# Sliding-window attention: transposes of the probabilities issued singly between the dense chunk's last matmuls, and VectorE's normalising moved ahead of the next maxima

## The reference, cut to what matters

```python
def sink_softmax(s, sink):
    m = jnp.maximum(jnp.max(s, axis=-1, keepdims=True), sink)
    e = jnp.exp(s - m)
    return e / (jnp.sum(e, axis=-1, keepdims=True) + jnp.exp(sink - m))

def swa_prompt(q, k, v, rel_bias, sinks):
    ...
    sc = jnp.einsum('bcqkgd,bcjkd->bckgqj', qc, k_band, preferred_element_type=jnp.float32) * SCALE
    sc = sc + rel_bias_heads(rel, rel_bias)
    ...
    p = sink_softmax(sc, sinks.astype(jnp.float32).reshape(SWA_KV_HEADS, SWA_GROUP, 1, 1))
    o = jnp.einsum('bckgqj,bcjkd->bcqkgd', p.astype(v.dtype), v_band)
```

## Time before, and the profile before

| what | value |
|---|---|
| median of 3 runs | 1555.41 us (1554.9 to 1557.6) |
| the profiled execution, first to last instruction | 1553.1 us |
| TensorE busy | 1495.8 us (96%) |
| VectorE busy | 1020.4 us (66%) |
| ScalarE busy | 607.5 us (39%) |
| GpSimd busy | 611.0 us (39%) |
| share of the chain that ended last | TensorE 80%, VectorE 9%, DMA 3%, GpSimd 3%, ScalarE 2% |

### The profile page before, as it was taken

The page is one execution under the profiler, slowest core; times in us unless marked ns, Lnnn a source line. Parts: engine busy times, 40 slices in busy tenths (PEclk is TensorE's granted clock), DMA queues, the critical chain, the costliest instruction groups (busy, mean ns, idle before and its releaser), DMA issues.

```text
span 1553.1 us, 25753 instructions
## 1 busy us (share of the span) xinstructions
PE 1495.8 (96%) x9803; PEld 1397.5 (90%) x9803; DVE 1020.4 (66%) x2016; ACT 607.5 (39%) x1256; POOL 611.0 (39%) x407
## 2 busy tenths in 40 slices
PE   6999999999999999999999999999999999999997
PEld 5889999999997998899788999999999999778885
DVE  6866667767674357867445896555555555578986
ACT  5143534435342235666223333333333332444463
POOL 6522232222222322225231568888888781000104
PEclk9999999999999999999999999999999999999999
DMA  6232222222132721129431122222222228723568
GB/s 199 63 94 74 74 87 65 73 70 70 30 97 75 233 95 38 56 82 291 156 108 58 45 67 86 83 83 83 70 83 68 71 83 278 240 97 116 170 195 156
DMA packets 156475, 165.41 MB, mean 107 GB/s; under 512 B 14005, under 2 KB 121913, under 8 KB 156353
## 3 DMA queue, kind: packets, MB, share of 16 engines
q1 hardware_dynamic: 119689, 109.34, 22.6%
q10 hardware_dynamic: 34840, 51.14, 10.0%
q0 software_dynamic: 1824, 3.28, 1.5%
HBM read 125.56 MB, written 39.85 MB: 107 GB/s over the span
## 4 chain that ended last, share of the span: by engine, by line
PE 80%; DVE 9%; DMA 3%; POOL 3%; ACT 2%; issue 2%; ACTq 1%; SPq 0%; DVEq 0%; POOLq 0%
PE bank L1138 16%; PE bank L1140 16%; PE bank L1139 16%; PE bank L1144 6%; PE bank L1146 6%; PE bank L1145 6%; PE bank L1170 4%; PE bank L1279 2%; PE bank L1250 1%; PE bank L1249 1%; DVE p L2649 1%; DVE rowsn L2408 1%; DVE p L2625 1%; POOL ring_l L1080 1%; PE bank L1629 1%
## 5 line engine op out<-in xcount | busy, mean ns | idle before, releaser
L1138 PE MATMUL bank<-ht_h,ring_h 128*128 128x352 f32 x816 | 268.9, 330 | 1.8 <-POOL ring_l L961 1.1
L1140 PE MATMUL bank<-ht_h,ring_l 128*128 128x352 f32 x816 | 263.2, 323 | 0.0
L1139 PE MATMUL bank<-ht_l,ring_h 128*128 128x352 f32 x816 | 262.6, 322 | 0.0
L960 POOL TENSOR_TENSOR ring_h<-raw,att 128x1024 fp32r<-128x1024 f32 x42 | 86.5, 2059 | 405.6 <-PE bank L1140 396.8
L1138 PE MATMUL bank<-m_h,ring_h 128*128 128x264 f32 x648 | 184.2, 284 | 1.2 <-DVE m_l L2895 1.2
L1139 PE MATMUL bank<-m_l,ring_h 128*128 128x264 f32 x648 | 184.2, 284 | 0.0
L1140 PE MATMUL bank<-m_h,ring_l 128*128 128x264 f32 x648 | 183.9, 284 | 0.0
L1138 PEld LDWEIGHTS bank<-ht_h,ring_h 128*128 128x128 f32 x816 | 153.8, 189 | 5.3 <-issue 2.0
L1139 PEld LDWEIGHTS bank<-ht_l,ring_h 128*128 128x128 f32 x816 | 154.6, 189 | 0.7
L1140 PEld LDWEIGHTS bank<-ht_h,ring_l 128*128 128x128 f32 x816 | 153.9, 189 | 0.0
L1138 PE MATMUL bank<-tb_h,ring_h 128*128 128x264 f32 x456 | 129.9, 285 | 0.2 <-DVE u2s L2909 0.2
(11 more groups left out here) (383 smaller groups left out, 3844.9 us busy)
## 6 DMA issues: line engine op xcount, KB each, us to landing
raw<-in_w_up SPq DMA_DIRECT2D x44, 512.0 KB, 3.9
raw<-in_w_in SPq DMA_DIRECT2D x34, 512.0 KB, 3.9
rb<-in_w_down SPq DMA_DIRECT2D x66, 256.0 KB, 2.9
d_y<-conv SPq DMA_DIRECT2D x22, 529.0 KB, 3.3
d_gate<-gst ACTq DMA_DIRECT2D x48, 176.0 KB, 1.9
a<-d_y SPq DMA_DIRECT2D x33, 256.0 KB, 6.1
ra<-d_y SPq DMA_DIRECT2D x33, 256.0 KB, 3.1
gm<-d_gate ACTq DMA_DIRECT2D x8, 528.0 KB, 4.4
```

Source lines behind the costliest of these rows:

```text
L960: order.link(nc.gpsimd.tensor_tensor(high, src, zero.to_broadcast(list(src.shape)), ALU.add))
L1138: nc.tensor.matmul(out, wh, xh, start=start, stop=False, skip_group_check=onto)
L1139: nc.tensor.matmul(out, wh, xl, start=False, stop=False, skip_group_check=onto)
L1140: return nc.tensor.matmul(out, wl, xh, start=False, stop=stop, skip_group_check=onto)
```

## The change

Two things change. TensorE no longer issues the turns of unit `s - 1` as a block behind the dense chunk: each single transpose of them follows one of the last matmuls of the chunk, 8 of 24 (4 where a unit has one key tile), from the 17th matmul on. The transposes of the sample keys follow the 9th matmul of step 6. VectorE's `sw_normalise(s - 1)` stands at the head of step `s`, ahead of `sw_maxima(s)` and the lows of unit `s - 2`, where it stood behind both. The dense chunk's loop is written out for it; its matmuls and their order among themselves are the same.

```diff
+            def dense_chunk(n, c, k_tiles=KT, xh=ht_h, xl=ht_l, col=0, q=None, turn=no_turn):
...
                 for k in range(k_tiles):
-                    mm = three(bank[q % 3][:, 0:CH], wh[:, k, col:col + P], wl[:, k, col:col + P],
-                               xh[:, k, CH * c:CH * c + CH], xl[:, k, CH * c:CH * c + CH],
-                               k == 0, k == k_tiles - 1)
-                mm.then_inc(chunk_full, 1)
+                    nc.tensor.matmul(out, wh[:, k, col:col + P], xh[:, k, sl], start=k == 0, stop=False)
+                    turn(3 * k)
+                    nc.tensor.matmul(out, wh[:, k, col:col + P], xl[:, k, sl], start=False, stop=False)
+                    turn(3 * k + 1)
+                    mm = nc.tensor.matmul(out, wl[:, k, col:col + P], xh[:, k, sl], start=False, stop=k == k_tiles - 1)
+                    if k == k_tiles - 1:
+                        mm.then_inc(chunk_full, 1)
+                    turn(3 * k + 2)
...
-            def sw_transposes(j):
+            def sw_turn(j, n):
+
                 g, qb = SWU[j]
-                pe.wait_ge(p_ready, U_SW + j + 1)
-                assert ti[0] == SW_TI[j]
-                for k in range(2 - SW_T[qb]):
-                    transposes(lambda b: [(b[:, P * h:P * h + P], p4[:, qb % 2, h, P * k:P * k + P]) for h in range(4)])
+                k, h = divmod(n, 4)
+                if n == 0:
+                    assert ti[0] == SW_TI[j]
+                    pe.wait_ge(p_ready, U_SW + j + 1)
+                if h == 0:
+                    pe.wait_ge(t_free, SW_TI[j] + k - 1)
+                mm = nc.tensor.transpose(tbank(SW_TI[j] + k)[:, P * h:P * h + P], p4[:, qb % 2, h, P * k:P * k + P], ident)
+                if h == 3:
+                    mm.then_inc(t_full, 1)
+                    ti[0] += 1
...
+                tiles = 4 * sw_turns(s - 1) if 1 <= s <= len(SWU) and s - 1 != SMP_J else 0
+
+                def sw_chunk_turn(m):
+
+                    if s == KW_STEP and m == 8:
+                        sw_key_turn()
+                    if 24 - tiles <= m:
+                        sw_turn(s - 1, m - 24 + tiles)
+
...
             for s in range(SW_STEPS):
                 if s == NT - 1:
                     sample_queries()
+                if s - 1 == SMP_J:
+                    sample_normalise()
+                elif 1 <= s <= len(SWU):
+                    sw_normalise(s - 1)
                 if s == SMP_J:
                     sample_maxima()
...
-                if s - 1 == SMP_J:
-                    sample_normalise()
-                elif 1 <= s <= len(SWU):
-                    sw_normalise(s - 1)
```

More of the change, by code:

```diff
@@ L1146, in three_moving, with no_turn @@
                 return nc.tensor.matmul(out, tl, wh, start=False, stop=stop, skip_group_check=onto)
-            def dense_chunk(n, c, k_tiles=KT, xh=ht_h, xl=ht_l, col=0, q=None):
+            def no_turn(m):
+                return
+            def dense_chunk(n, c, k_tiles=KT, xh=ht_h, xl=ht_l, col=0, q=None, turn=no_turn):
                 q = position(n, c) if q is None else q
@@ L1155, in dense_chunk @@
                 wl = flat(ring_l[:, s]).rearrange("p (k c) -> p k c", k=k_tiles)
+                out, sl = bank[q % 3][:, 0:CH], slice(CH * c, CH * c + CH)
                 for k in range(k_tiles):
-                    mm = three(bank[q % 3][:, 0:CH], wh[:, k, col:col + P], wl[:, k, col:col + P],
-                               xh[:, k, CH * c:CH * c + CH], xl[:, k, CH * c:CH * c + CH],
-                               k == 0, k == k_tiles - 1)
-                mm.then_inc(chunk_full, 1)
+                    nc.tensor.matmul(out, wh[:, k, col:col + P], xh[:, k, sl], start=k == 0, stop=False)
[6 more added lines that the diff above has]
+                    turn(3 * k + 2)
             ti = [0]
@@ L1382, in sw_scores, with sw_key_turn @@
                     mm.then_inc(s_full, 1)
-            def sw_transposes(j):
+            def sw_turn(j, n):
                 g, qb = SWU[j]
-                pe.wait_ge(p_ready, U_SW + j + 1)
-                assert ti[0] == SW_TI[j]
-                for k in range(2 - SW_T[qb]):
-                    transposes(lambda b: [(b[:, P * h:P * h + P], p4[:, qb % 2, h, P * k:P * k + P]) for h in range(4)])
+                k, h = divmod(n, 4)
[8 more added lines that the diff above has]
+                    ti[0] += 1
+            def sw_key_turn():
+                pe.wait_ge(smp_in, 16 * 10)
+                transposes(lambda b: [(b[:, 0:P], kwn[:, 0, :]), (b[:, P:P + DEC], kwn[0:DEC, 1, :])])
             def sw_values(j):
@@ L1436, in _ @@
                     sw_values(s - 3)
-                for n, c in sw_fillers(s):
+                tiles = 4 * sw_turns(s - 1) if 1 <= s <= len(SWU) and s - 1 != SMP_J else 0
[4 more added lines that the diff above has]
+                        sw_turn(s - 1, m - 24 + tiles)
+                chunks = sw_fillers(s)
+                for n, c in chunks[:-1]:
                     dense_chunk(n, c)
-                if s == KW_STEP:
-                    pe.wait_ge(smp_in, 16 * 10)
-                    transposes(lambda b: [(b[:, 0:P], kwn[:, 0, :]), (b[:, P:P + DEC], kwn[0:DEC, 1, :])])
+                dense_chunk(*chunks[-1], turn=sw_chunk_turn)
                 if s - 1 == SMP_J:
                     sample_transposes()
-                elif 1 <= s <= len(SWU):
-                    sw_transposes(s - 1)
             pe.wait_ge(ot_done, 2)
```

## The result

Eight runs of the changed kernel have a median of 1561.28 us (1558.27 to 1565.3); eight of the kernel before, beside them, 1555.16 (1554.55 to 1557.61). The ratio is 1.0034, with a 95% interval of 1.0021 to 1.0048: slower, by a little more than the 0.2% that can be told from no change. A second measurement gave 1560.10 (12 runs) beside 1556.47 (35 runs of before), a ratio of 1.0027, 1.0014 to 1.0041.

The account below looks back on a forecast made before the run. TensorE, busy 132.7 of the sliding part's 141 us, waited 7.1 us for VectorE's normalising, held by GpSimd. The terms 3.5 + 0.6 + 0.7 - 0.8 gave +4.0 on 1555.4, so 1559.4 us; range 1554.0 to 1563.0.

Parts of the forecast that it names:

- signs: Profile after: unit 1's maxima at about 567.6, two waits in step 2, waits about 11 us, merge 4 us later.
- The transposes' own cost: Transposes issued singly between the chunk's matmuls: no cheaper than in the burst, 0.10 to 0.11 us each, so 0.
- The rival that they would cost 0.06: Transposes' loads hidden, 6 us gross won, low-half waits grow 2.5: 1555.9, no change; chance 0.28 with the tally's low end.
- The first steps: Start of the sliding part: unit 1's maxima slip behind late normalising, waits of 4.7 us where 1.2 stood, +3.5 us.
- Step 4: GpSimd's subtraction may hold the moved normalising, delaying the low half: TensorE waits 0 to 1.3 us, taken as 0.6.
- Step 7: At the sample's query copies (L2680): TensorE's wait of 2.02 us becomes 2.5 to 2.9, taken as +0.7 us.
- The later steps: Remaining waits of steps 3, 10, 12 and 15, 3.9 us: change of -2.2 to +0.9, taken as -0.8 us.
- another slow stretch: Half clock after new long waits in steps 2, 11 and 12: one costs 1.5 us, 1560.9, two 1562.4; chance 0.17.
- The rival on the other side: From step 3 on the bigger room carries VectorE's delays, 5.9 us of waits and the slow stretch go: 1551.5; chance 0.12.

Follow-up runs that it names:

- the cleanest pair: The kernel before and the changed kernel, both with GpSimd subtracting only 32 columns of each weight slab and query half: 1549.00 us and 1552.59 us.

## Why the prediction was right, and which terms were off

The forecast was 1559.4, or +4.0 over the median of before, and the measurement gave 1561.28, and 1560.10 the second time: +6.1 over the 1555.16 beside it and +3.6, inside the range, and the chance of 0.60 stood on slower. Of its signs most came: the maxima of unit 1 start at 570.31, or 567.6 once the 2.7 us are taken off by which the sliding part began later; TensorE waits twice in step 2, the second time for the low half; the waits add up to 12.3 us where some 11 were said; the sliding part is 4.3 longer. By its steps:

- *The transposes' own cost, 0.* In step 6 of the changed kernel eight lone transposes stand 0.273 us apart (599.44 to 601.35 in seven), with a matmul of 0.16 between two: 0.113 each, against 0.10 to 0.11 in the burst. The rival that they would cost 0.06 is dead; they are dearer by a trifle. A step without a wait takes 6.59 to 6.62 us from score to score with the burst and 6.63 to 6.65 with single transposes, 0.03 a step, so 0.3 (the cleanest pair) to 0.5 for all of them. The full kernels' sliding parts leave some 1 us (131.1 without waits, against 130.2 without waits and slow stretch in before). The other half lies at the waits: a step loses some 0.2 more than the wait that is listed (step 4 takes 8.13, less 1.30 is 6.83, where a step without a wait has 6.63), and the changed kernel has ten of them, before seven with the one behind the key turn. The forecast put both at nothing.
- *The first steps, +3.5.* Measured: 1.73 + 0.94 + 1.26 + 0.60 = 4.5 where 1.4 stood in before (1.23 and 0.16, the latter in step 3, which the forecast counted with the later steps), +3.1. I had said 1.7 + 1.0 + 1.4 + 0.6. The waits are right; their cause only in part, since the old order would still wait 4.1 in steps 1 to 3.
- *Step 4, 0.6 of 0 to 1.3.* It was the upper end, 1.30: GpSimd's subtraction at 587.23 caught the normalising, which took 3.31 us instead of 1.14 in the timeline of after:

```profile
586.73 3.31 DVE L2676 TENSOR_SCALAR p<-p,att 128x256 f32<-128x256 f32 x4
587.23 2.39 POOL L1011 TENSOR_TENSOR ring_l<-raw,ring_h 128x1024 fp32r<-128x1024 f32 x1 [23.89 <-ACT ring_h L1698]
```

- *Step 7, +0.7.* Measured 2.83 against 2.02: +0.8.
- *The later steps, -0.8.* Measured 0.31 + 1.26 + 1.82 + 0.19 = 3.6 against 1.92 + 0.72 + 1.06 = 3.7: -0.1 (-0.3 with the 0.16 of step 3, as the forecast counted). This term and step 4 were mis-sized by most, 0.5 to 0.7 us each. Step 15 went as I said, 0.19; step 12 did not, as GpSimd's row moved along and met the maxima there again, and the normalising of step 11 took 4.22 us beside four query operations.

With these the sum is 3.1 + 1.3 + 0.8 - 0.1 + 0.3 to 1.0, less the 0.3 of a wait behind the key turn that went: 5.1 to 5.8, and the runs of equal clock show 5.3, or 4.4 to 6.0 by the rows of the table. That the medians are nearer to my 4.0 is luck and no merit of the sum: it was 1 to 2 us too low, and the clock gave back about 1.5. There I had the sign wrong. I gave 0.17 to another slow stretch in the new waits of steps 2, 11 and 12; none followed those in the two profiles of the changed kernel, and the kernel runs at a slightly higher mean clock than before.

The rival on the other side, that the bigger room would carry all of VectorE's delays, fell as its working said it could: with GpSimd's work cut the later waits do go, and with it they do not. The room of a step grew from 0.23 to 1.1, but a held operation of VectorE costs up to 2.2.

## What to carry to other kernels

Work that moves to an earlier slot needs its inputs earlier by the same amount: compare that with the room of the quietest step, before looking at any stall (here 1.1 us against a room of 0.23, and a loss of 8 us by the medians, 11.5 in the sliding part, without the second edit). An edit in the order of one engine's rows moves the other engines' rows with it, so a stall that comes of two of them meeting is moved rather than removed; take away one of the two parties instead, as with the copies given to an idle engine. And measure the kernel before as a variant too, and compare runs of equal clock where less than a per cent counts: here the clock took about a quarter off the cost at equal clock.

## What the runs showed of the hardware

- VectorE's operations between SBUF tiles are held one by one while an instruction of GpSimd runs: 3.81 us for four operations beside a whole subtraction, 2.63 beside one cut in four, 0.88 alone; and 3.4 against 1.4 us for eight copies. With the pieces the two engines take turns, 0.56 to 0.78 us for each of VectorE's operations beside 0.72 to 0.74 for each piece. The Trainium skill, "SBUF — State Buffer", section "Who interferes with whom", says that the two share a port pair as an exclusive lock that is held for a whole instruction; these rows agree with it.
- The half-clock stretch behind a wait of TensorE is not a fixed property of the kernel: the same wait of 2.83 to 2.85 us was followed by one in one execution of the changed kernel and by none in another; of the sixteen waits of 1.90 to 2.85 us in the 14 profiles ten were followed by one.
- A transpose of 128 columns alone between matmuls of 352 costs TensorE 0.113 us, the same within 0.01 as in a burst of eight. The Trainium skill, "TensorE: Matmul & The Clock Gate", section "Back-to-back issue gap", has 81 ns for a matmul of 128 columns with its weight load in a sustained stream and about 56 ns for an isolated one; these runs show more than either.
